# The decay mask of a Mamba-2 scan moved from ScalarE's bias and a masked score to eight VectorE instructions, with the ScalarE, VectorE and TensorE order around it rewritten

## The chip, the cores and the metric

The kernel runs on one core of a Trainium2 chip. A core has five engines that work at the same time: TensorE (PE; its weight loads are shown apart as PEld), VectorE (DVE), ScalarE (ACT), GpSimd (POOL) and SyncE (SP), which here only issues DMAs. Each engine takes its instructions in order and waits on semaphores for the others. The metric is the device time of one execution in microseconds (us). Lower is better.

## The reference, cut to what matters

The program is a chain of layers over 512 tokens of width 1024 in float32: a gated delta net, a chunked attention, two convolutional FFNs, an S5 mixer, an MLP, then the Mamba-2 mixer (`_ssd_mixer`) and another MLP. The change touches the Mamba-2 mixer alone. It has 4 chunks of 128 tokens and 32 heads in 4 groups of 8:

```python
a_cs = jnp.cumsum(a_dt, axis=-1)
l_mat = jnp.exp(_segsum(a_dt))          # exp(cs[l] - cs[s]) for s <= l, else 0
cb = jnp.einsum('bclgn,bcsgn->bcgls', c_in, b_in)
y_diag = jnp.einsum('bcgls,bgrcls,bcsgrp->bclgrp', cb, l_mat, xdt)
decay_states = jnp.exp(a_cs[..., -1:] - a_cs)
states = jnp.einsum('bclgn,bgrcl,bclgrp->bcgrpn', b_in, decay_states, xdt)
...
y_off = jnp.einsum('bclgn,bcgrpn,bgrcl->bclgrp', c_in, prev, jnp.exp(a_cs))
y = y_diag + y_off + xs * d.astype(f32).reshape(G, R, 1)
y = y.reshape(bsz, L, M2_D_INNER) * jax.nn.silu(z.astype(f32))
yg = y.reshape(bsz, L, G, M2_D_INNER // G)
yg = yg * lax.rsqrt(jnp.mean(yg * yg, axis=-1, keepdims=True) + NORM_EPS)
```

## The kernel before, in words

Every float32 product with a weight is three TensorE passes: the weight is split into a high part (ScalarE, L209, `w_hi`) and the rest (GpSimd, L238 or L2534, `w_lo`, two instructions of 128x1024 for one slot of weights). Weights stream through two buffers; SyncE issues their loads.

The scan is written out by hand as 16 steps, v = 0 to 15, where g = v // 4 is the group of heads and c = v % 4 the chunk. "c = 0" below means the steps 0, 4, 8, 12. Each engine has its own list of these steps.

TensorE (`ssd_pe`), in step v: `z_half(v)`, one 128-column tile of the gate projection z (24 matmuls of 512 columns, into bank v % 2); `pre(v + 1)`, which transposes the next step's x and B (L2460, L2465) and makes its scores C times B (L2466); `main(v)`, the 16 or 8 small products with `lw` (L2477) and `cdec` (L2479); and, but for c = 3, the new state (L2486). Around these stand parts of the norm of the group before: `gnorm_sums_pe` (L2652), the sums of squares of two tiles, after main(v) for c = 2 and 3, and `gnorm_spread_pe` (L2667), which spreads 1/rms over the partitions, ahead of main(v) for c = 1.

VectorE (`ssd_dve`): `xdt` (L2599, x times dt); then the difference `lw` (L2603), one instruction over 128x1024 that takes the minimum of the row of cumulated sums (`g_row`, the same row in every partition) and the partition's own sum; the outputs of step v - 1 (L2576); a wait for ScalarE; the triangular mask on the scores (L2613, 128x128 in PSUM); `lw` times scores (L2615); the state update of step v - 1 (L2588 or L2591). With c = 0 it multiplies the group before by silu(z) (`gnorm_gate_dve`, L2639); with c = 1 it makes 1/rms and scales the group before that (`gnorm_scale_dve`, L2675).

ScalarE (`ssd_act`): `b_tok` (L2505), `cdec` = exp of g_row (L2510), then eight exps of 128x128 on `lw`, each with the negated sum of its head as bias column (L2514). In the odd steps it then takes silu of two z tiles (L2520), splits the next slot of weights (L209), and for c = 1 and 2 squares two tiles of the group before (L2645). The root of the mean (L2658) comes after the exps of c = 0. Exp, silu and sqrt are in different tables of ScalarE; a change of table shows as ACT_TABLE_LOAD. Copy and Square need no change.

GpSimd (`ssd_pool`): decay of the state (L2545), `xdec` (L2556), `cdec` times C (L2562), and in the even steps from 2 on the two instructions of the low part of a slot (L2534).

SyncE loads `g_row` for step v once step v - 2 has used it; the weights of the output projection (`m_out`) come behind the last of these loads in its queue.

The minimum works as a mask because the cumulated sums fall with the token: where the row's token lies before the partition's, the minimum keeps the exponent at zero or below, and the triangle on the scores clears the entry.

Of the kernel before, what the change touches and what calls it, by code (L numbers as in the profile page):

```python
# [22 lines left out]
ALU = mybir.AluOpType  # L23
ACT = mybir.ActivationFunctionType
# [58 lines left out]
def ge(eng, sem, value):  # L83

    if isinstance(value, int) and value <= 0:
        return
    eng.wait_ge(sem, value)
# [19 lines left out]
def build(nc, t, out):  # L107

    ctx = ExitStack()
    with ctx:  # L110
# [2147 lines left out]
        g_in = [sem(f"g_in{i}") for i in range(2)]  # L2258
        M_NCS = 0
        (M_X, M_ABS, M_E, M_U, M_L, M_DT, M_ADT, M_CS, M_EDX, M_DEC) = range(10)  # L2260
# [93 lines left out]
        def steps_sums_dve(dve):  # L2354
            dve.wait_ge(d_pe, 1)
            dve.tensor_scalar(mcols[:, M_NCS, :], bank[7][:, 0:128], -1.0, None, ALU.mult)
            dve.tensor_copy(mcols[:, M_CS, :], bank[7][:, 0:128]).then_inc(d_dve, 1)
            dve.tensor_copy(mcols[:, M_DEC, :], bank[7][:, 128:256]).then_inc(d_dve, 1)
            dve.wait_ge(d_dve, 4)
            dve.tensor_tensor(mcols[:, M_EDX, :], mcols[:, M_DEC, :], mcols[:, M_CS, :], ALU.subtract).then_inc(d_dve, 1)  # L2360
# [46 lines left out]
        def z_slot(i):  # L2407
            return SLOTS["m_in"] + M_XBC + i
# [28 lines left out]
        def ssd_pe(pe):  # L2437
# [15 lines left out]
            def pre(v):  # L2453
# [7 lines left out]
                mm.then_inc(m_xt, 1)  # L2461
                ge(pe, m_w, 2 * (v - 1))
                ge(pe, m_bt, carried(v - 1) if v >= 2 else 0)
# [4 lines left out]
            def main(v):  # L2468
                g, c = v // 4, v % 4
                pe.wait_ge(m_w, 2 * v + 2)  # L2470
                if c:
# [16 lines left out]
            for v in range(16):  # L2488
                z_half(v)
                if v < 15:  # L2490
                    pre(v + 1)
                if v >= 8 and v % 4 == 1:
                    gnorm_spread_pe(pe, v // 4 - 2)
                main(v)
                if v >= 4 and v % 4 >= 2:
                    gnorm_sums_pe(pe, v // 4 - 1, v % 4 - 2)

        def ssd_act(act):
            for v in range(16):
# [11 lines left out]
                act.wait_ge(m_dl, v + 1)  # L2511
                for k in range(8):
                    col = c * M_H + 8 * g + k
                    op = act.activation(lw[v % 2][:, k, :], lw[v % 2][:, k, :], ACT.Exp, bias=mcols[:, M_NCS, col:col + 1])  # L2514
                op.then_inc(m_le, 1)
                if v % 2:
                    for z in (v - 1, v):
                        act.wait_ge(gemm_ready, 2 * z_slot(0) + z + 1)
                        ge(act, m_yz, z - 3)
                        act.activation(zT[:, z % 4, :], bank[z % 2][:, :], ACT.Silu).then_inc(bank_free, 1)  # L2520
                    n = z_slot(v // 2 + 2)
                    split_hi(act, n, n % 2, landed(n - n % 2))
                if g and c in (1, 2):
                    gnorm_squares_act(act, g - 1, c - 1)
                if g >= 2 and c == 0:
                    gnorm_root_act(act, g - 2)

# [39 lines left out]
        def ssd_dve(dve):  # L2567
# [25 lines left out]
            for v in range(16):  # L2593
                g, c = v // 4, v % 4
                dve.wait_ge(m_xt, v + 1)
                if v >= 2:
# [5 lines left out]
                dve.wait_ge(g_in[v % 2], 16 * (v // 2 + 1))  # L2602
                dve.tensor_tensor(lw[v % 2][:, :, :], g_row[v % 2][:, :, :],  # L2603
                                  mcols[:, M_CS, c * M_H + 8 * g:c * M_H + 8 * g + 8].unsqueeze(2).to_broadcast([P, 8, P]),
                                  ALU.min).then_inc(m_dl, 1)
                if v:
                    outputs(v - 1)
                if g >= 2 and c == 1:
                    gnorm_rcp_dve(dve, g - 2)
                dve.wait_ge(m_le, v + 1)  # L2610
                dve.wait_ge(m_cb, v + 1)
                scores = C_BANK[v % 2][:, P:2 * P]
                dve.tensor_tensor(scores, scores, triu[:, :], ALU.mult).then_inc(m_w, 1)  # L2613
                dve.wait_ge(m_w, 2 * v + 1)
                dve.tensor_tensor(lw[v % 2][:, :, :], lw[v % 2][:, :, :],  # L2615
                                  C_BANK[v % 2][:, P:2 * P].unsqueeze(1).to_broadcast([P, 8, P]), ALU.mult).then_inc(m_w, 1)
                if v:
                    states(v - 1)
                if g and c == 0:
                    gnorm_gate_dve(dve, g - 1)  # L2620
                if g >= 2 and c == 1:
                    gnorm_scale_dve(dve, g - 2)
            outputs(15)
            gnorm_rcp_dve(dve, 2)
            gnorm_gate_dve(dve, 3)
# [57 lines left out]
        def gnorm_act(act):  # L2683
            gnorm_root_act(act, 2)
            act.wait_ge(gemm_ready, 2 * SLOTS["m_out"])
            gnorm_hi_act(act, 0, 8)
            gnorm_squares_act(act, 3, 0)
            gnorm_squares_act(act, 3, 1)
            gnorm_root_act(act, 3)
            gnorm_hi_act(act, 8, 8)  # L2690
# [14 lines left out]
        def m_out_pe(pe):  # L2705
# [30 lines left out]
            pe.wait_ge(bank_free, 2 * base)  # L2736
            for k in range(2):
                first_pair(0, k)
            gnorm_spread_pe(pe, 2)
            for k in range(2, 6):  # L2740
                first_pair(0, k)
            gnorm_sums_pe(pe, 3, 0)
            for k in range(6, KD):
                first_pair(0, k)
# [308 lines left out]
```

## Time and profile before

| | |
|---|---|
| median of 3 runs | 3025.12 us (3024.24 to 3026.7) |
| the profiled execution's own time | 3026.7 us |
| its span, first to last instruction | 3024.9 us |
| busy: PE | 2856.2 us (94%) |
| busy: DVE, ACT, POOL | 1579.0, 1049.1, 1224.4 us |
| mean granted TensorE clock | 0.955 of full speed |
| the scan's 16 steps | about 2388 to 2548 us of the span |

Between the profiled execution's own time and its span lie 1.8 us at the two ends. Stretches are told in microseconds from the span's start. A busy share is an average over the whole program; what a change in the scan is worth is read from the stretch of the scan, and there from what TensorE waits for.

### The profile page before, as it was taken

The numbers are of one execution on the slowest core, as the hardware profiler recorded it, in microseconds if no ns is written. First come the engines' busy times: TensorE is split into PE (matmuls) and PEld (weight loads), VectorE is DVE, ScalarE is ACT, GpSimd is POOL, SyncE is SP. The second block draws the span as 40 slices with busy tenths as digits, with TensorE's granted clock in tenths as the row PEclk, the third lists the DMA queues.
The fourth block names the chain that finished last, engine by engine and source line by source line (L and its number), as shares of the span: only waits on it lengthen the run. The fifth ranks groups of instructions, "written<-read, shape, count | busy, mean of one in ns | idle before, by whom it ended". The sixth has DMA issues, their size and how long they took to land.

```text
span 3024.9 us, 38804 instructions
## 1 busy us (share of the span) xinstructions
PE 2856.2 (94%) x14541; PEld 2345.6 (78%) x14541; DVE 1579.0 (52%) x2180; ACT 1049.1 (35%) x1425; POOL 1224.4 (40%) x556
## 2 busy tenths in 40 slices
PE   7999999999998998999998789999999998999998
PEld 6867886788877865788886677888878787778887
DVE  4435655676768447564556626555354465242224
ACT  4331222333333246333333212222224666232222
POOL 3433432344444420344443214444433566544443
PEclk9998998999999989999998779999999999999999
DMA  4320000335532320455533732655322332223322
GB/s 133 94 76 22 1 1 14 112 95 148 154 116 85 111 99 29 137 171 170 189 117 116 236 101 83 236 195 181 98 83 87 111 107 77 84 84 98 98 98 70
DMA packets 343960, 326.43 MB, mean 108 GB/s; under 512 B 28816, under 2 KB 320144, under 8 KB 343696
## 3 DMA queue, kind: packets, MB, share of 16 engines
q1 hardware_dynamic: 309760, 257.34, 27.4%
q10 hardware_dynamic: 34064, 67.18, 6.3%
q8 instruction: 97, 1.59, 0.2%
q14 instruction: 39, 0.32, 0.0%
HBM read 303.44 MB, written 21.04 MB: 107 GB/s over the span
## 4 chain that ended last, share of the span: by engine, by line
PE 72%; DVE 6%; issue 3%; ACT 3%; POOL 1%; DMA 0%; ACTq 0%; DVEq 0%; SPq 0%; POOLq 0%
PE bank L248 18%; PE bank L250 18%; PE bank L249 18%; PE bank L262 3%; PE bank L267 3%; PE bank L263 3%; PE bank L1923 1%; PE bank L1918 1%; PE bank L1347 1%; PE bank L363 1%; DVE xt L406 0%; DVE sq_x L333 0%; PE bank L679 0%; PE bank L2652 0%; PE bank L2477 0%
## 5 line engine op out<-in xcount | busy, mean ns | idle before, releaser
L238 POOL TENSOR_TENSOR w_lo<-w_raw,w_hi 128x1024 fp32r<-128x1024 f32 x400 | 1009.3, 2545 | 1459.6 <-ACT w_hi L209 1444.1
L248 PE MATMUL bank<-x_hi,w_hi 128*128 128x512 f32 x2032 | 799.8, 394 | 12.7 <-POOL w_lo L238 7.8
L249 PE MATMUL bank<-x_lo,w_hi 128*128 128x512 f32 x2032 | 793.3, 390 | 0.0
L250 PE MATMUL bank<-x_hi,w_lo 128*128 128x512 f32 x2032 | 793.2, 390 | 0.0
L209 ACT ACTIVATE w_hi<-w_raw 128x2048 fp32r<-128x2048 f32 x208 | 398.1, 1914 | 892.5 <-PE bank L250 792.0
L248 PEld LDWEIGHTS bank<-x_hi,w_hi 128*128 128x128 f32 x2032 | 383.3, 189 | 96.9 <-issue 15.2
L249 PEld LDWEIGHTS bank<-x_lo,w_hi 128*128 128x128 f32 x2032 | 383.4, 189 | 81.0 <-issue 2.2
L250 PEld LDWEIGHTS bank<-x_hi,w_lo 128*128 128x128 f32 x2032 | 383.1, 189 | 80.3
L248 PE MATMUL bank<-m_hi,w_hi 128*128 128x512 f32 x384 | 149.6, 390 | 0.0
L250 PE MATMUL bank<-m_hi,w_lo 128*128 128x512 f32 x384 | 149.4, 389 | 0.0
L249 PE MATMUL bank<-m_lo,w_hi 128*128 128x512 f32 x384 | 149.4, 389 | 0.0
L1212 DVE SCALAR_TENSOR_TENSOR y_gate<-bank,par,y_gate 128x511 f32<-128x511 f32 x88 | 66.0, 750 | 155.6 <-ACT y_gate L1146 153.9
L2231 DVE SCALAR_TENSOR_TENSOR h<-bank,mod,h 128x512 f32<-128x512 f32 (+1 forms) x64 | 47.4, 749 | 183.0 <-PE bank L250 166.1
L2210 DVE SCALAR_TENSOR_TENSOR m_r<-bank,m_r 128x512 f32<-128x512 f32 x64 | 43.8, 684 | 178.4 <-ACT m_r L2163 178.4
L1062 DVE SCALAR_TENSOR_TENSOR ada_acc<-ada_w,cond,ada_acc 128x1024 f32<-128x1024 f32 (+1 forms) x84 | 119.7, 1425 | 1.6
L2214 DVE TENSOR_TENSOR m_lo<-m_r,m_hi 128x512 fp32r<-128x512 f32 (+1 forms) x64 | 78.9, 1233 | 52.2 <-ACT m_hi L2165 52.2
L248 PE MATMUL bank<-act_hi,w_hi 128*128 128x512 f32 x264 | 103.2, 391 | 0.0
L250 PE MATMUL bank<-act_hi,w_lo 128*128 128x512 f32 x264 | 102.7, 389 | 0.0
L249 PE MATMUL bank<-act_lo,w_hi 128*128 128x512 f32 x264 | 102.7, 389 | 0.0
L262 PE MATMUL bank<-x_hi,w_hi 128*128 128x512 f32 x176 | 79.6, 452 | 18.3 <-ACT x_hi L373 8.1
L574 DVE SCALAR_TENSOR_TENSOR qkvz<-bank,par,qkvz 128x511 f32 (+2 forms) x72 | 53.8, 749 | 77.4 <-ACT qkvz L544 67.8
L838 POOL TENSOR_TENSOR X<-Rm,lev 128x512 f32<-128x512 f32 x56 | 70.3, 1270 | 54.4 <-PE bank L784 47.8
(436 smaller groups left out, 4642.3 us busy)
## 6 DMA issues: line engine op xcount, KB each, us to landing
w_raw<-in_mlp_w SPq DMA_DIRECT2D x128, 512.0 KB, 4.5
ada_w<-in_ada_w ACTq DMA_DIRECT2D x96, 512.0 KB, 4.9
w_raw<-in_f_w_up SPq DMA_DIRECT2D x88, 512.0 KB, 5.1
w_raw<-in_m_w_in SPq DMA_DIRECT2D x40, 512.0 KB, 4.7
w_raw<-in_a_w_in SPq DMA_DIRECT2D x32, 512.0 KB, 4.7
w_raw<-in_f_w_down SPq DMA_DIRECT2D x32, 512.0 KB, 4.0
w_raw<-in_w_kv SPq DMA_DIRECT2D x16, 512.0 KB, 4.3
w_raw<-in_s_w_glu SPq DMA_DIRECT2D x16, 512.0 KB, 5.4
```

The lines of the kernel that those rows point to most:

```text
L209: act.activation(w_hi[s][:, :], w_raw[s][:, :], ACT.Copy).then_inc(hi_done, 1)
L238: op = pool.tensor_tensor(w_lo[s][:, part], w_raw[s][:, part], w_hi[s][:, part].bitcast(F32), ALU.subtract)
L248: pe.matmul(dst, hi_l, hi_r, start=start, stop=False)
L249: pe.matmul(dst, hi_l, lo_r, start=False, stop=False)
L250: return pe.matmul(dst, lo_l, hi_r, start=False, stop=stop)
L262: pe.matmul(bank[o][:, :], w_hi[0][:, cols[o]], rhs_hi[:, k, :], start=(k == 0), stop=False)
L263: pe.matmul(bank[o][:, :], w_lo[0][:, cols[o]], rhs_hi[:, k, :], start=False, stop=False)
L267: mm = pe.matmul(bank[o][:, :], w_hi[0][:, cols[o]], rhs_lo[:, k, :], start=False, stop=(k == kt - 1))
L838: pool.tensor_tensor(X2[s][:, :, :], Rm[s][:, :, :], bc4(lev[:, l, :]), ALU.mult).then_inc(da_mask, 1)
L1062: dve.scalar_tensor_tensor(acc, ada_w[k][:, :, :], cond[:, k:k + 1], acc, ALU.mult, ALU.add).then_inc(ada_used, 1)
L1212: dve.scalar_tensor_tensor(y[:, s, d:T], bank[2 * s + o][:, 0:T - d], pcol("f_conv", i + (3 * 44 * f + 44 * (2 - d) + col + F_START[c] + s ...
L2214: dve.tensor_tensor(lo, m_r[:, o, :], m_hi[:, ds(2 * i + (2 * s + o), 1), :].bitcast(F32), ALU.subtract).then_inc(p_lo, 1)
```

## The change

The mask goes into the exponent. VectorE takes, head by head, row minus the head's own sum plus `upmask` (0 on and above the diagonal, -1e30 below), eight instructions of 128x128, and ScalarE then needs one exp of 128x1024 with no bias. The minimum, the triangle on the scores and the column of negated sums (`M_NCS`) go. The order of the rest changes too: silu of z is taken in every step, not for two tiles in every other; the squares' sums on TensorE stand after main(v) of c = 1 and 2; root, reciprocal and spread of the group before stand at the end of c = 3; scale and gate stand together in c = 0; and the first products of the output projection no longer hold a spread.

```diff
 def steps_sums_dve(dve):
-    dve.tensor_scalar(mcols[:, M_NCS, :], bank[7][:, 0:128], -1.0, None, ALU.mult)
...
 ssd_pe, in step v
-                if v >= 8 and v % 4 == 1:
-                    gnorm_spread_pe(pe, v // 4 - 2)
                 main(v)
-                if v >= 4 and v % 4 >= 2:
-                    gnorm_sums_pe(pe, v // 4 - 1, v % 4 - 2)
+                if v >= 4 and v % 4 in (1, 2):
+                    gnorm_sums_pe(pe, v // 4 - 1, v % 4 - 1)
+                if v >= 4 and v % 4 == 3:
+                    gnorm_spread_pe(pe, v // 4 - 1)
...
 ssd_act, in step v
                 act.wait_ge(m_dl, v + 1)
-                for k in range(8):
-                    col = c * M_H + 8 * g + k
-                    op = act.activation(lw[v % 2][:, k, :], lw[v % 2][:, k, :], ACT.Exp, bias=mcols[:, M_NCS, col:col + 1])
-                op.then_inc(m_le, 1)
+                act.activation(lw[v % 2][:, :, :], lw[v % 2][:, :, :], ACT.Exp).then_inc(m_le, 1)
+                act.wait_ge(gemm_ready, 2 * z_slot(0) + v + 1)
+                ge(act, m_yz, v - 3)
+                act.activation(zT[:, v % 4, :], bank[v % 2][:, :], ACT.Silu).then_inc(bank_free, 1)
                 if v % 2:
-                    for z in (v - 1, v):
-                        act.wait_ge(gemm_ready, 2 * z_slot(0) + z + 1)
-                        ge(act, m_yz, z - 3)
-                        act.activation(zT[:, z % 4, :], bank[z % 2][:, :], ACT.Silu).then_inc(bank_free, 1)
                     n = z_slot(v // 2 + 2)
                     split_hi(act, n, n % 2, landed(n - n % 2))
                 if g and c in (1, 2):
                     gnorm_squares_act(act, g - 1, c - 1)
-                if g >= 2 and c == 0:
-                    gnorm_root_act(act, g - 2)
+                if g and c == 3:
+                    gnorm_root_act(act, g - 1)
...
 ssd_dve, in step v
-                dve.tensor_tensor(lw[v % 2][:, :, :], g_row[v % 2][:, :, :],
-                                  mcols[:, M_CS, c * M_H + 8 * g:c * M_H + 8 * g + 8].unsqueeze(2).to_broadcast([P, 8, P]),
-                                  ALU.min).then_inc(m_dl, 1)
+                for k in range(8):
+                    op = dve.scalar_tensor_tensor(lw[v % 2][:, k, :], g_row[v % 2][:, k, :],
+                                                  mcols[:, M_CS, c * M_H + 8 * g + k:c * M_H + 8 * g + k + 1], upmask[:, :],
+                                                  ALU.subtract, ALU.add)
+                op.then_inc(m_dl, 1)
                 if v:
                     outputs(v - 1)
-                if g >= 2 and c == 1:
-                    gnorm_rcp_dve(dve, g - 2)
                 dve.wait_ge(m_le, v + 1)
                 dve.wait_ge(m_cb, v + 1)
-                scores = C_BANK[v % 2][:, P:2 * P]
-                dve.tensor_tensor(scores, scores, triu[:, :], ALU.mult).then_inc(m_w, 1)
-                dve.wait_ge(m_w, 2 * v + 1)
                 dve.tensor_tensor(lw[v % 2][:, :, :], lw[v % 2][:, :, :],
                                   C_BANK[v % 2][:, P:2 * P].unsqueeze(1).to_broadcast([P, 8, P]), ALU.mult).then_inc(m_w, 1)
                 if v:
                     states(v - 1)
-                if g and c == 0:
+                if v >= 4 and c == 0:
+                    if g >= 2:
+                        gnorm_scale_dve(dve, g - 2)
                     gnorm_gate_dve(dve, g - 1)
-                if g >= 2 and c == 1:
-                    gnorm_scale_dve(dve, g - 2)
+                if g and c == 3:
+                    gnorm_rcp_dve(dve, g - 1)
             outputs(15)
-            gnorm_rcp_dve(dve, 2)
...
 gnorm_act
-            gnorm_root_act(act, 2)
...
 m_out_pe
-            for k in range(2):
-                first_pair(0, k)
-            gnorm_spread_pe(pe, 2)
-            for k in range(2, 6):
+            for k in range(4):
                 first_pair(0, k)
             gnorm_sums_pe(pe, 3, 0)
-            for k in range(6, KD):
+            for k in range(4, KD):
                 first_pair(0, k)
```

The waits on `m_w` count one increment for each step in place of two.

## Rows read from the trace of the kernel before

**Rows 1.** The waits, 2385 to 2590 us: who waited for whom, us, times, longest.

```profile
DVE bank L2613 <- ACT lw L2514: 47.7, 16, 5.6
...
PEld bank L2477 <- DVE lw L2615: 5.9, 3, 3.6
...
PE bank L2477 <- DVE prev L2591: 5.5, 4, 3.4
```

**Rows 2.** Timeline of TensorE: start, us, engine, line, output and inputs, count.

```profile
2413.91 0.45 PE L2477 MATMUL bank<-lw,xdt 128*64 128x128 f32 x4
...
2423.15 0.45 PE L2477 MATMUL bank<-lw,xdt 128*64 128x128 f32 x4
...
2431.53 1.09 PE L2477 MATMUL bank<-lw,xdt 128*64 128x128 f32 x16
...
2439.85 0.45 PE L2477 MATMUL bank<-lw,xdt 128*64 128x128 f32 x4
...
2452.82 1.84 PE L2652 MATMUL bank<-ones,sq 128*128 128x1 f32 x16
...
2479.69 1.06 PE L2667 MATMUL bank<-ident,ncol 128*128 128x128 f32 x8
...
2533.35 0.45 PE L2477 MATMUL bank<-lw,xdt 128*64 128x128 f32 x4 [3.40 <-DVE prev L2591]
```

**Rows 3.** Timeline of ScalarE, steps 5 and 6.

```profile
2437.05 1.28 ACT L2520 ACT_TABLE_LOAD   x1
2438.35 0.60 ACT L2520 ACTIVATE zT<-bank 128x512 f32<-128x512 f32 x1
...
2439.68 1.91 ACT L209 ACTIVATE w_hi<-w_raw 128x2048 fp32r<-128x2048 f32 x1
2441.48 1.14 ACT L2645 ACTIVATE sq<-xbc 128x512 f32<-128x512 f32 x2
...
2444.10 1.06 ACT L2510 ACTIVATE cdec<-g_row 128x1024 f32<-128x1024 f32 x1
2445.07 2.43 ACT L2514 ACTIVATE lw<-lw,mcols 128x128 f32<-128x128 f32 x8
```

**Rows 4.** Timeline of VectorE, in steps 4, 6 and 9.

```profile
2430.33 2.49 DVE L2639 SCALAR_TENSOR_TENSOR xbc<-xbc,zT 128x512 f32<-128x512 f32 x4
...
2439.62 0.69 DVE L2599 TENSOR_TENSOR xdt<-bank,mcols 128x512 f32<-128x512 f32 x1 [0.39 <-PE bank L2460]
2440.23 1.22 DVE L2603 TENSOR_TENSOR lw<-g_row,mcols 128x1024 f32<-128x1024 f32 x1
...
2447.53 0.30 DVE L2613 TENSOR_TENSOR bank<-bank,triu 128x128 f32<-128x128 f32 x1 [4.51 <-ACT lw L2514]
2447.87 1.22 DVE L2615 TENSOR_TENSOR lw<-lw,bank 128x1024 f32<-128x1024 f32 x1
...
2480.79 2.72 DVE L2675 SCALAR_TENSOR_TENSOR xbc<-xbc,par,bank 128x512 f32<-128x512 f32 x4 [2.02 <-PE bank L2667]
```

**Rows 5.** Timeline of GpSimd, in step 6.

```profile
2442.95 1.04 POOL L2556 TENSOR_TENSOR xdec<-xdt,mcols 128x512 f32<-128x512 f32 x1
2445.24 2.40 POOL L2562 TENSOR_TENSOR cdec<-cdec,xbc 128x1024 f32<-128x1024 f32 x1 [1.25 <-ACT cdec L2510]
```

**Rows 6.** Timelines of VectorE, then GpSimd, in the S5 tables, 966 to 1003 us.

```profile
970.53 2.39 DVE L1771 SCALAR_TENSOR_TENSOR tab<-tab,scol 128x64 f32<-128x64 f32 x1
972.85 2.43 DVE L1772 SCALAR_TENSOR_TENSOR tab_tmp<-tab,scol 128x64 f32<-128x64 f32 x1
...
977.14 0.29 DVE L1771 SCALAR_TENSOR_TENSOR tab<-tab,scol 128x128 f32<-128x128 f32 x1
977.35 0.28 DVE L1772 SCALAR_TENSOR_TENSOR tab_tmp<-tab,scol 128x128 f32<-128x128 f32 x1
...
970.45 4.74 POOL L238 TENSOR_TENSOR w_lo<-w_raw,w_hi 128x1024 fp32r<-128x1024 f32 x2 [20.31 <-ACT w_hi L209]
```

**Rows 7.** The chain that ended last, 2370 to 2620 us: start, us, what.

```profile
2515.60 7.45 DMA w_raw<-in_m_w_out
```

More of the change, by code:

```diff
@@ L2258, in build @@
         g_in = [sem(f"g_in{i}") for i in range(2)]
-        M_NCS = 0
         (M_X, M_ABS, M_E, M_U, M_L, M_DT, M_ADT, M_CS, M_EDX, M_DEC) = range(10)
@@ L2461, in pre @@
                 mm.then_inc(m_xt, 1)
-                ge(pe, m_w, 2 * (v - 1))
+                ge(pe, m_w, v - 1)
                 ge(pe, m_bt, carried(v - 1) if v >= 2 else 0)
@@ L2469, in main @@
                 g, c = v // 4, v % 4
-                pe.wait_ge(m_w, 2 * v + 2)
+                pe.wait_ge(m_w, v + 1)
                 if c:
```

## The prediction, made before the changed kernel was run

> **What bounds the kernel now.** I read the page first: TensorE is busy 94% of the span, so in the scan I asked only what TensorE waits for. The waits of that stretch [rows 1] show the large number on VectorE, 47.7 us of waiting for ScalarE's exps, and small ones on TensorE: 5.5 us in four places for the updated state and, at three of the same places, 5.9 us for `lw`. So the long wait of VectorE is nearly all hidden behind `z_half`. The timeline of TensorE gives the undisturbed period of a step, main to main [rows 2]: 9.24 us for c = 2 to 3 (2413.91 to 2423.15), 8.38 for c = 3 to 0, 8.32 for c = 0 to 1. I take 9.24 for c = 1 to 2 also. From group 1 on come two sums of 1.7 to 1.8 us and one spread of some 0.9. The waits lie in steps 6, 7, 10, 11, 14 and 15, where the starts of main are 6 to 6.5 us late in all, against these periods; 3.4 of it stand ahead of main(14) [rows 2], behind a weight load that the chain shows as 7.45 us [rows 7]. At most about 6 us can be won inside the scan.
>
> **The change part by part.** The eight exps took 2.43 us; one exp over 128x1024 has its nearest row in `cdec`, 1.06 [rows 3]: 1.4 us less on ScalarE. The mask goes: 0.34 us from its start to that of the product [rows 4]. The negated column is one small VectorE instruction, once, some 0.3 us by the mask's row, and nothing waits closely for it.
>
> The difference costs more. A pair of `scalar_tensor_tensor` of 128x128 with both tensors in SBUF stands at 977.14 and 977.35 [rows 6]: 0.21 us apart, the last 0.29, so eight take 7 x 0.21 + 0.29 = 1.76 us, against 1.22 [rows 4]. If nothing else acts, `lw` times scores is ready 1.4 + 0.34 - 0.54 = 1.2 us earlier in each step.
>
> Something else acts. At 970.45 GpSimd starts two w_lo instructions, 4.74 us together. VectorE's two instructions of 128x64, with no wait between them in the code, then take 2.39 and 2.43 us in place of some 0.2: the first stands until GpSimd's first is over, and the second until GpSimd's second is over [rows 6]. They take turns, one instruction each. One long instruction loses one such turn; eight short ones can lose a turn to every instruction that GpSimd has ready. The Trainium skill ("SBUF — State Buffer", "SBUF: two separate sides") says that a VectorE instruction with two SBUF inputs and a GpSimd instruction that reads SBUF exclude each other for the whole instruction, whichever starts first; it doesn't say who gets the port at a boundary between short ones. The trace agrees on the exclusion.
>
> What GpSimd has ready comes from its order. `xdec`, 1.04 us, is released by the xdt just ahead of the difference; `cdec` takes 2.40 [rows 5], a w_lo pair 4.74. I place the turns, from measured durations.
>
> Steps with c = 1: xdec, then cdec: difference 1.76 + 1.04 + 2.40 = 5.2 us. In step 5 the way from the product of step 4 is the four gates (2.4), xdt (0.6), difference (5.2), exp (1.1), product (1.25) and state (0.65), 11.1 us in all [rows 3, 4], against a period of 8.32: TensorE waits 2.8. In steps 9 and 13 the scale now stands there too, 2.6: 13.7 against 8.32, 5.4 us each. Sum 13.6.
>
> Steps 4, 8, 12: xdec and both w_lo: 1.76 + 1.04 + 4.74 = 7.5 us, and with exp and product main is ready 10.1 us after the difference starts. In steps 8 and 12 the difference also starts late, since VectorE now waits for the root: ScalarE does silu (0.5), the split (1.9), a table load (1.3) and the root (0.3) first [rows 3]. I get waits of 3.1, 3.1, and 2.1 in step 4. Sum 8.3.
>
> Steps 0 and 3: one w_lo in step 0; the decay of the state and cdec in step 3 between the short ones: 1.35 and 1.5. Sum 2.9.
>
> The spread: it needs root and reciprocal, about 4.4 us after the silu of z, which starts 0.66 ahead of main; so 3.75 after main's start, and main takes 2.0: 1.75 us of waiting in steps 7 and 11. In step 15 it lies ahead of the first y_lo, which starts some 8 us after main(15) in either kernel, and is hidden. Sum 3.5.
>
> Step 13: the squares stand behind the split of the late weight load [rows 3, 7], and their sums now come before z_half(14): 0.8. In return the old wait at main(14) goes.
>
> Moved sums and spreads: one pair of sums (1.8) is now ahead of main(15) that stood in cover behind it, and one spread (0.9) leaves the output projection: +0.9.
>
> The sum: 13.6 + 8.3 + 2.9 + 3.5 + 0.8 + 0.9 - 6.3 (the old waits) = +23.7 us. The profiled execution took 3026.7, so 3050.4; it is 1.6 above the median of the runs, so 3049 us for the median, about 0.8% slower. GpSimd's own work is unchanged; ScalarE saves 1.4 x 16 = 22 us and pays up to 16 more table loads of 1.3 us, 21 us, in places where it otherwise waits.
>
> Table loads: the trace has 1.28 us for the load and 1.30 from its start to that of the silu behind it [rows 3]. The Trainium skill ("ScalarE: Activation LUTs", "What ACT_TABLE_LOAD costs") counts about 2.66 us for a switch, with a drain of 1.38. By that figure root and spread would come 1.4 us later in steps 7 and 11, an estimate of 3 us more. The trace has no such drain, and the sum goes by its row.
>
> Bounds of the unknown terms. Where each turn falls: if no turn is lost the waits of steps 0, 3, 4 and 5 vanish and those of 8, 9, 12 and 13 too (the way in step 9 is 13.7 - 3.4 = 10.3 from product to main, and the earlier product leaves it in cover), which takes off 24.8. If a second cdec or w_lo turn falls into two more steps it adds 2.4 each. TensorE's clock: after idle time it can fall to the lower of its two levels; 3.4 us ahead of main(14) left it at full speed, and 5.4 is longer than that. What lies ahead of a drop I bound by none and by 2 us for each of steps 9 and 13.
>
> **The rivals.** (1) No change that can be told. The eight short instructions hold the port like one. For it: they are issued back to back with no wait, and the difference is only 0.54 us longer then. Against it: the pair at 970.53 had no wait between them either and lost a turn each. Then the sum is 23.7 - 24.8 = -1: 3024 us.
>
> (2) Faster. ScalarE's order decides: with exps 1.4 us shorter and squares a step earlier, the waits of steps 6, 7, 10, 11, 14 and 15 go, 6.3 us, the spread leaves the projection, 0.9, and root and reciprocal come in time. Place: steps 7 and 11, where the root would have to be done by main's end. Price: -7.2, 3018 us. It decides if turns are kept and the way from silu to spread is under 2.7 us; against it stand 4.4 from the rows.
>
> (3) Slower by half of it: GpSimd wins a turn only when its next instruction is already queued, as at 970.45 (a pair), and not with a fresh xdec or cdec. Then the c = 0 steps keep their waits in part and c = 1 lose them: about 8.3 + 3.5 + 0.8 + 0.9 - 6.3 plus 2 for step 9 and 13, +9: 3034 us.
>
> **How the numbers follow.** The turns as I placed them: 0.60, 3049 us, own range 3040 to 3060. (3): 0.20, 3029 to 3040. (1): 0.13. (2): 0.07. A change under about 0.2%, 6 us, can't be told from none by this measurement. Faster 0.07; same 0.13; a tenth of (3) would fall into it too, so 0.15; slower 0.78. The range leaves out (2) and half of (1) below, 0.07 and 0.06, and 0.05 above: 3024 to 3060.
>
> **What the profile of the changed kernel would show.** The instructions of `lw<-g_row,mcols,upmask`, 128 of them, with 0.29 us as their least and some of 1.3 and 2.6 us, between which xdec, cdec or w_lo of GpSimd run; the difference as a whole near 5 us for c = 1 and 7.5 for c = 0. One exp of 1.06. TensorE waiting for `lw` or the state of steps 3, 4, 5, 8, 9, 12 and 13, longest at 9 and 13, and 1.7 us ahead of the spread in steps 7 and 11; no wait ahead of main(14). About 16 more table loads. The start of the output projection some 22 us later than 2549. If the 128 instructions all take 0.29, the turns are wrong and the time is near that of before; if waits ahead of the spread are missing too, (2) holds. The prediction is also wrong where GpSimd's work falls at other times than I placed it, since two steps of lateness move which instruction is ready.

## The result, and the profile after

| | before | after |
|---|---|---|
| median of the runs compared | 3024.68 us (3022.64 to 3026.7, 4 runs) | 3058.62 us (3050.95 to 3060.2, 4 runs) |
| the profiled execution's own time | 3026.7 us | 3054.83 us |
| its span | 3024.9 us | 3053.0 us |
| from the first `xdt` of the scan to the first `h` of the output projection | 194.69 us | 225.90 us |

The ratio is 1.0108, with a 95% interval of 1.0096 to 1.0119: the change makes the kernel 1.1% slower, by 29 to 36 us. All 31 runs on record of the kernel after have a median of 3057.39 us (3050.95 to 3061.96), so the 33.9 us between the two medians of the table, which the text below uses, may be some 1 us too large. 3049 us had been predicted, in a range of 3024 to 3060. The last row of the table is the part of the program that the change touches, measured in the two traces; it grew by 31.2 us. The span grew by 28.1 only, because the part ahead of the scan, whose code is the same, was 4.05 us shorter in this execution (the first `xdt` starts at 2384.44 and not at 2388.49). For the scan I therefore compare this stretch and not the span; it is called the scan time below.

The page of the kernel after, its span and the busy times:

```profile
span 3053.0 us, 38801 instructions
PE 2869.6 (94%) x14541; PEld 2357.7 (77%) x14541; DVE 1620.6 (53%) x2275; ACT 1044.9 (34%) x1327; POOL 1212.2 (40%) x556
```

TensorE is as busy as before, 94%, and gained only 13 us of busy time. VectorE gained 42 us. So I asked again what TensorE waits for. The waits of the kernel after, 2381 to 2611 us (who waited for whom: us, times, longest):

```profile
ACT lw L2510 <- DVE lw L2598: 40.7, 10, 6.6
...
PEld bank L2475 <- DVE lw L2606: 19.6, 7, 4.0
...
DVE lw L2606 <- ACT lw L2510: 13.5, 5, 5.5
...
PE bank L2475 <- DVE prev L2582: 10.7, 4, 3.8
...
PE bank L2475 <- DVE lw L2606: 6.9, 3, 2.7
...
PEld bank L2659 <- DVE ncol L2654: 6.2, 3, 2.6
```

In [rows 1] VectorE waited 47.7 us for ScalarE; now ScalarE waits 40.7 us for VectorE's difference. TensorE's matmuls waited 5.5 us for the state, in four places; now 10.7 for the state and 6.9 for `lw`, and its weight loads, which stand just ahead of them, 19.6 for `lw` in place of 5.9. The spread, which did not wait [rows 2], waits three times, in the steps 7, 11 and 15.

The difference itself, by the instructions that touch `lw` (x count: shortest, median, longest in ns):

```profile
L2598 DVE SCALAR_TENSOR_TENSOR lw<-g_row,mcols,upmask x128: 336/343/2485, 2385.0 to 2563.0; 128x128 f32<-128x128 f32 x128
L2510 ACT ACTIVATE lw<-lw x16: 1038/1057/1064, 2390.5 to 2564.1; 128x1024 f32<-128x1024 f32 x16
```

The median of the 128 short instructions is 0.343 us and the longest 2.485, about GpSimd's product for `cdec` [rows 5]. Each of the 16 exps takes the 1.06 us that was expected. The timelines of VectorE and GpSimd show the turns. Step 8, then step 9:

```profile
2470.16 7.24 DVE L2598 SCALAR_TENSOR_TENSOR lw<-g_row,mcols,upmask 128x128 f32<-128x128 f32 x8
...
2485.30 5.09 DVE L2598 SCALAR_TENSOR_TENSOR lw<-g_row,mcols,upmask 128x128 f32<-128x128 f32 x8
...
2493.85 2.18 DVE L2598 SCALAR_TENSOR_TENSOR lw<-g_row,mcols,upmask 128x128 f32<-128x128 f32 x8
```

```profile
2470.32 1.08 POOL L2550 TENSOR_TENSOR xdec<-xdt,mcols 128x512 f32<-128x512 f32 x1 [9.35 <-DVE xdt L2593]
2471.36 4.84 POOL L2528 TENSOR_TENSOR w_lo<-w_raw,w_hi 128x1024 fp32r<-128x1024 f32 x2
...
2485.46 1.08 POOL L2550 TENSOR_TENSOR xdec<-xdt,mcols 128x512 f32<-128x512 f32 x1 [9.26 <-DVE xdt L2593]
2487.57 2.41 POOL L2556 TENSOR_TENSOR cdec<-cdec,xbc 128x1024 f32<-128x1024 f32 x1 [1.02 <-ACT cdec L2508]
```

In step 10 (2493.85) GpSimd starts nothing until the last of the eight is under way (its next instruction starts at 2495.66): 2.18 us. In step 9 xdec and cdec fall between them: 5.09, and in step 8 xdec and the two w_lo: 7.24. The prediction had 5.2 and 7.5 for these two kinds.

What it does to TensorE (its timeline):

```profile
2442.48 0.45 PE L2475 MATMUL bank<-lw,xdt 128*64 128x128 f32 x4 [2.79 <-DVE prev L2582]
...
2469.67 1.16 PE L2659 MATMUL bank<-ident,ncol 128*128 128x128 f32 x8 [1.56 <-DVE ncol L2654]
...
2479.80 1.09 PE L2475 MATMUL bank<-lw,xdt 128*64 128x128 f32 x16 [2.70 <-DVE lw L2606]
...
2493.59 0.45 PE L2475 MATMUL bank<-lw,xdt 128*64 128x128 f32 x4 [3.80 <-DVE prev L2582]
...
2549.35 3.28 PE L2644 MATMUL bank<-ones,sq 128*128 128x1 f32 x16 [1.74 <-ACT sq L2637]
...
2560.66 0.45 PE L2475 MATMUL bank<-lw,xdt 128*64 128x128 f32 x4
```

From one main to the next, by their starts, the periods in us are:

| step to next | 0 | 1 | 2 | 3 | 4 | 5 | 6 | 7 | 8 | 9 | 10 | 11 | 12 | 13 | 14 |
|---|---|---|---|---|---|---|---|---|---|---|---|---|---|---|---|
| before | 8.31 | 9.14 | 9.24 | 8.38 | 8.32 | 10.09 | 11.36 | 10.17 | 9.21 | 9.49 | 11.19 | 10.17 | 9.21 | 12.61 | 11.18 |
| after | 8.72 | 9.13 | 10.35 | 9.91 | 11.17 | 12.56 | 11.05 | 13.71 | 13.79 | 10.89 | 11.05 | 13.71 | 13.80 | 17.62 | 10.27 |

The columns 5, 9 and 13 of the kernel after also hold a pair of sums (1.8 us) that stood two steps later before. The losses stand where the prediction put them (at main(3) to main(5), main(8), main(9), main(12) and main(13)) and in one place where it had almost none: between main(13) and main(14), 17.62 us.

### The profile page after: what moved, and what is told of

Same layout as the page of the kernel before. It is cut to its first block, busy times and chain, and to the rows that moved or that the text cites. A ratio compares the mean times of both kernels' runs of the same rounds, so it can differ in the third digit from the quotient of the medians.

```text
span 3053.0 us, 38801 instructions
## 1 busy us (share of the span) xinstructions
PE 2869.6 (94%) x14541; PEld 2357.7 (77%) x14541; DVE 1620.6 (53%) x2275; ACT 1044.9 (34%) x1327; POOL 1212.2 (40%) x556
## 4 chain that ended last, share of the span: by engine, by line
PE 70%; DVE 8%; issue 3%; ACT 2%; DMA 0%; POOL 0%; ACTq 0%; DVEq 0%; SPq 0%; POOLq 0%
PE bank L248 18%; PE bank L250 18%; PE bank L249 18%; PE bank L262 3%; PE bank L267 3%; PE bank L263 3%; DVE lw L2598 1%; PE bank L1923 1%; PE bank L1918 1%; PE bank L1347 1%; PE bank L363 1%; PE bank L2644 1%; DVE xt L406 0%; PE bank L679 0%; DVE sq_x L333 0%
## 5 line engine op out<-in xcount | busy, mean ns | idle before, releaser
L238 POOL TENSOR_TENSOR w_lo<-w_raw,w_hi 128x1024 fp32r<-128x1024 f32 x400 | 1007.3, 2540 | 1455.4 <-ACT w_hi L209 1439.9
```

Source lines behind the costliest of these rows:

```text
L238: op = pool.tensor_tensor(w_lo[s][:, part], w_raw[s][:, part], w_hi[s][:, part].bitcast(F32), ALU.subtract)
```

## The experiments

All medians are set against runs of the kernel before on the same chip. The scan time is that of each profiled execution.

| kernel | median, us | less before | ratio (95%) | scan time less that of before |
|---|---|---|---|---|
| after | 3058.62 | +33.9 | 1.0108 (1.0096 to 1.0119) | +31.2 |
| old order, new arithmetic | 3036.26 | +9.9 | 1.0040 (1.0027 to 1.0052) | +10.5 |
| new order, old arithmetic | 3036.43 | +10.1 | 1.0038 (1.0024 to 1.0052) | +13.4 |
| after, GpSimd held back | 3034.27 | +7.9 | 1.0028 (1.0018 to 1.0038) | +11.2 |
| after, two long instructions | 3041.13 | +14.8 | 1.0052 (1.0035 to 1.0068) | +16.6 |
| after, mask in PSUM | 3032.05 | +6.6 | 1.0018 (1.0009 to 1.0027) | +10.2 |
| after, early load | 3053.80 | +28.4 | 1.0087 (1.0071 to 1.0102) | +27.8 |
| after, held back, early load | 3027.70 | +2.3 | 1.0006 (0.9996 to 1.0015) | +2.8 |
| the same, and an early root | 3019.69 | -5.6 | 0.9978 (0.9969 to 0.9988) | -3.3 |
| old order, new arithmetic, held back | 3020.68 | -4.8 | 0.9984 (0.9975 to 0.9994) | -2.6 |
| the same, and early load | 3019.00 | -6.3 | 0.9980 (0.9970 to 0.9990) | -2.8 |
| before, early load alone | 3020.45 | -4.8 | 0.9985 (0.9976 to 0.9994) | -3.3 |

### The turns: GpSimd held back by one wait

```diff
 ssd_pool, in step v, behind the decay of the state, ahead of xdec
+                pool.wait_ge(m_dl, v + 1)
```

> The changed kernel with one more wait: in each step GpSimd starts xdec, cdec and the weights' low part only once the eight short VectorE instructions of the difference are done. Nothing is computed otherwise. Theory T (turns: each short instruction loses the port to a GpSimd instruction that is ready): all but the first of the eight go back to about 0.2 us apart, the difference takes 1.8 us in most steps, TensorE's waits of 2.7 to 3.8 us in steps 5, 8, 9, 12 and 13 go, and the time falls by some 25 to 32 us, to 3023 to 3031. Rival O (the new order with its root, spread, scale, gate and table loads costs the time): GpSimd's work is only later, the time stays at 3050 or above. Rival L (the eight instructions' own length, 1.8 in place of 1.2 us): it stays too, since there are still eight.

It took 3034.27 us. Against before that is +7.9 us in place of +33.9: 26 us given back by the medians, and 20.0 by the scan times of the two traces. The instructions of VectorE and GpSimd are the same; only the time at which GpSimd starts is another. VectorE's timeline of this kernel in step 9, then GpSimd's:

```profile
2474.63 2.17 DVE L2599 SCALAR_TENSOR_TENSOR lw<-g_row,mcols,upmask 128x128 f32<-128x128 f32 x8
```

```profile
2476.89 1.05 POOL L2551 TENSOR_TENSOR xdec<-xdt,mcols 128x512 f32<-128x512 f32 x1 [5.13 <-DVE lw L2599]
2477.89 2.37 POOL L2557 TENSOR_TENSOR cdec<-cdec,xbc 128x1024 f32<-128x1024 f32 x1
```

The difference now takes 2.17 in step 9 and 2.18 in step 8, and the periods 7 to 8 and 8 to 9 fall from 13.71 and 13.79 to 10.93 and 9.74. That is the turns. The result lies 3 us above the top of what I had expected, and the trace says where: the period 13 to 14 is not shorter but longer, 18.79. The wait has a price of its own: `cdec` is now late at two mains, 2.7 us in all.

### Is it the port? The mask from PSUM

```diff
+            for b in range(2):
+                dve.tensor_copy(C_BANK[b][:, 2 * P:3 * P], upmask[:, :]).then_inc(m_mk, 1)
...
 ssd_dve, in step v
+                dve.wait_ge(m_cb, v + 1)
+                if c < 3:
+                    dve.wait_ge(m_bt, carried(v) + 1)
                 for k in range(8):
                     op = dve.scalar_tensor_tensor(lw[v % 2][:, k, :], g_row[v % 2][:, k, :],
-                                                  mcols[...], upmask[:, :],
+                                                  mcols[...], C_BANK[v % 2][:, 2 * P:3 * P],
                                                   ALU.subtract, ALU.add)
```

A copy of the mask stands in unused columns of the two score banks. The two waits keep VectorE from reading a bank that TensorE is writing. GpSimd's order is that of the kernel after.

> The changed kernel with its mask read from PSUM: a copy of upmask stands in the free columns of the two score banks, so that each of the eight short instructions has one tensor in SBUF and one in PSUM. GpSimd's order isn't touched; the difference now waits for the scores and b_tok of its step. T (two SBUF inputs are what makes VectorE and GpSimd exclude each other): no turn is lost, the eight take 2.1 to 2.5 us in every step while GpSimd's xdec and cdec run beside them at 1.04 and 2.4 us, and the time is near that of the hold, 3028 to 3038. Rival P (it is the number of short instructions, or their semaphores, that costs): no gain, 3055.

It took 3032.05 us: +6.6 in place of +33.9, 27 us given back by the medians and 21.0 by the scan times. The instructions on `lw` in this kernel, then VectorE's difference of step 9, then GpSimd in the same stretch:

```profile
L2607 DVE SCALAR_TENSOR_TENSOR lw<-g_row,mcols,bank x128: 336/343/349, 2383.7 to 2539.9; 128x128 f32<-128x128 f32 x128
```

```profile
2470.94 2.15 DVE L2607 SCALAR_TENSOR_TENSOR lw<-g_row,mcols,bank 128x128 f32<-128x128 f32 x8
```

```profile
2471.10 1.04 POOL L2552 TENSOR_TENSOR xdec<-xdt,mcols 128x512 f32<-128x512 f32 x1 [4.28 <-DVE xdt L2599]
2473.20 2.40 POOL L2558 TENSOR_TENSOR cdec<-cdec,xbc 128x1024 f32<-128x1024 f32 x1 [1.06 <-ACT cdec L2510]
```

xdec runs in the middle of the eight, as in the kernel after, and neither loses anything: the longest of 128 instructions falls from 2485 to 349 ns. The same instruction with one of its two tensors in PSUM does not take turns with GpSimd. The Trainium skill ("SBUF — State Buffer", "SBUF: two separate sides") names two SBUF inputs as a condition for the exclusion; this run agrees. The two added waits cost this kernel something too: in six steps VectorE's difference waits for `b_tok`, 16.4 us in all; in step 9, shown here, it does not.

### Few long instructions in place of many short ones

```diff
-                for k in range(8):
-                    op = dve.scalar_tensor_tensor(..., ALU.subtract, ALU.add)
-                op.then_inc(m_dl, 1)
+                dve.tensor_tensor(lw[v % 2][:, :, :], g_row[v % 2][:, :, :], mcols[...].to_broadcast([P, 8, P]),
+                                  ALU.subtract).then_inc(m_d1, 1)
+                dve.wait_ge(m_d1, v + 1)
+                dve.tensor_tensor(lw[v % 2][:, :, :], lw[v % 2][:, :, :],
+                                  upmask[:, :].unsqueeze(1).to_broadcast([P, 8, P]), ALU.add).then_inc(m_dl, 1)
```

> The changed kernel with its difference in two long instructions in place of eight short ones: subtract the own sums over 128x1024, then add the mask over 128x1024. The same values, 2.4 us of VectorE alone in place of 1.8, but only two turns to lose. T: in a c = 1 step the difference takes 2.4 + 1.0 (xdec) = 3.5 us in place of 5.1, in c = 0 about 3.5 to 5.8 in place of 7.2; the time is 8 to 20 us below the changed kernel, 3036 to 3048. L: longer arithmetic makes it slower than the changed kernel, by up to 0.6 us a step: 3060 or more. O: no change or slightly slower.

It took 3041.13 us, +14.8 in place of +33.9: 19 us given back by the medians and 14.6 by the scan times, though without contention two instructions of 1.22 us are longer than the eight together. VectorE's timeline, step 9:

```profile
2476.46 1.21 DVE L2598 TENSOR_TENSOR lw<-g_row,mcols 128x1024 f32<-128x1024 f32 x1
2477.70 1.95 DVE L2602 TENSOR_TENSOR lw<-lw,upmask 128x1024 f32<-128x1024 f32 x1
```

From start to end this is 3.19 us, against 5.09. GpSimd gets one turn between the two, and its work waits in return (that xdec stands at 1.96 us in place of 1.04). So in this kernel the loss goes with the number of boundaries between VectorE's instructions, not with the work.

### Order and arithmetic apart

The kernel before with the new difference and the one exp, and without the mask on the scores; the order of all engines is the old one:

```diff
-                dve.tensor_tensor(lw[v % 2][:, :, :], g_row[v % 2][:, :, :], mcols[...].to_broadcast([P, 8, P]), ALU.min).then_inc(m_dl, 1)
+                for k in range(8):
+                    op = dve.scalar_tensor_tensor(lw[v % 2][:, k, :], g_row[v % 2][:, k, :], mcols[...], upmask[:, :], ALU.subtract, ALU.add)
+                op.then_inc(m_dl, 1)
```

> The kernel before with the arithmetic of the change alone: eight short instructions with the mask, one exp, no triangle on the scores; the order of all engines as before. T: turns are lost here as well (the difference takes about 5 us for c = 1 and 7 for c = 0), but scale and gate stand in different steps and VectorE doesn't wait for the root, so most of it lies in cover: waits of 1 to 2 us in steps 3, 4, 5, 10 and 14, less about 3 us that shorter exps save: +2 to +8 us against the kernel before, 3027 to 3033. O: the arithmetic saves 1.2 us a step on the way to main, so the time is 3 to 6 us below before. L: about +1.

The other half, the new order with the minimum, eight exps and the mask on the scores:

```diff
 ssd_act, in step v
+                act.wait_ge(gemm_ready, 2 * z_slot(0) + v + 1)
+                ge(act, m_yz, v - 3)
+                act.activation(zT[:, v % 4, :], bank[v % 2][:, :], ACT.Silu).then_inc(bank_free, 1)
...
-                if g >= 2 and c == 0:
-                    gnorm_root_act(act, g - 2)
+                if g and c == 3:
+                    gnorm_root_act(act, g - 1)
```

> The changed kernel with the arithmetic of before: one minimum, eight exps with bias, triangle on the scores; the order of the change. T: only the spread's waits (1.6 us in steps 7 and 11) and some 1.6 us in steps 9 and 13 are added, and moved sums: +4 to +10 us against before, 3029 to 3035. O: nearly all of the loss is here, +25 or more, 3050. L: as T.

They took 3036.26 and 3036.43 us: each half costs about 10. Both came out above what was expected, the arithmetic by 2 to 3 us and the order at the very edge of its range; the difference of the arithmetic alone took 7.06 us in step 3 and 7.24 in step 4. Together the halves make 20 and the whole change 33.9; by the scan times they make 23.9 and the whole 31.2. The periods show where the 7.3 us between these two come from:

| step to next | 7 | 8 | 11 | 12 | 13 |
|---|---|---|---|---|---|
| before | 10.17 | 9.21 | 10.17 | 9.21 | 12.61 |
| new arithmetic, old order | 10.17 | 11.00 | 10.17 | 11.00 | 12.30 |
| old arithmetic, new order | 10.91 | 10.97 | 10.90 | 10.99 | 16.24 |
| after | 13.71 | 13.79 | 13.71 | 13.80 | 17.62 |

In the old order the 7.2 us of step 8 lie in cover (10.17, as before). The new order lets VectorE wait for 1/rms and gives it scale and gate in the same step, so the cover is used up, and each further microsecond of VectorE is one of TensorE. In the periods 7, 8, 11 and 12 the whole change costs 7.7 us more than the two halves added up. The medians differ by more, 14; no row shows the other 6 us.

### The arithmetic with the old order, held back

```diff
 the kernel before with the new arithmetic, ssd_pool, ahead of xdec
+                pool.wait_ge(m_dl, v + 1)
```

> The kernel before, with the arithmetic of the change and GpSimd held until the difference is done; the order of the other engines as before. T: the difference takes 2.2 us in place of 1.2, exp 1.4 less, the mask 0.3 less, no turns; main(6), (7), (10), (11) and (15) start without their waits of 0.3 to 1.1 us, main(14) 1.7 us earlier, step 0 0.8 later: 2 to 5 us below the kernel before. L: no gain, within 1 us of it.

3020.68 us, 4.8 below before, as expected; its scan time is 2.6 less. The new arithmetic is a gain, if a small one, once the turns are gone.

### The long period 13 to 14: the late weight load

The chain that ended last, in the kernel after (start, us, what); then ScalarE's timeline:

```profile
2539.86 0.32 SPq L2422
...
2540.51 0.40 SPq L171
...
2541.10 5.66 DMA w_raw<-in_m_w_out
...
2548.59 0.62 ACT sq L2637
```

```profile
2546.78 1.91 ACT L209 ACTIVATE w_hi<-w_raw 128x2048 fp32r<-128x2048 f32 x1 [3.94 <-DMA w_raw<-in_m_w_out]
2548.59 1.13 ACT L2637 ACTIVATE sq<-xbc 128x512 f32<-128x512 f32 x2
```

SyncE takes the load of `g_row` for step 15 (L2422) only when the difference of step 13 has ended, and the weights of the output projection stand behind it. The difference of step 13 ends 5.09 us after it starts, late, so the load, the split and the squares come late, and TensorE waits 1.74 us for the squares. The chain after it has z matmuls of 0.43 us in place of 0.23, and the windows show the granted clock (of each stretch: us, busy times, then the clock, the DMA share and GB/s):

```profile
2540.00:2550.00 10.00, 5.22 (x39) 4.28 (x39) 6.51 (x19) 6.01 (x8) 2.04 (x2) 0.81 0.80 262
2550.00:2560.00 10.00, 10.00 (x38) 8.48 (x38) 1.82 (x2) 4.47 (x4) 7.06 (x3) 0.68 0.01 2
```

The edit that tests it puts the first load of the output projection ahead of the `g_row` loads of steps 14 and 15 in SyncE's queue:

```diff
+            sp_slot(sp, z_slot(8), halves(rows_k(t["m2_w_out"][0]), 0, 0, KD, 0))
...
-            sp_slots(sp, SLOTS["m_out"], 8, lambda i, s: halves(w, s, (i - s) * P, KD, KD * s))
+            (the same loads, without the first)
```

> The changed kernel with one load moved in SyncE's queue: the first slot of the output projection's weights ahead of the g_row loads of steps 14 and 15, in place of behind them. Theory T2 (the late load is what makes step 13 to 14 take 17.6 us in place of 11: it stands behind the g_row load of step 15, and that waits for the difference of step 13): the split of step 13 no longer waits, step 13 to 14 falls to about 11 to 12 us, the clock doesn't fall there, and the time is 5 to 7 us below the changed kernel, 3050 to 3053. Rival: the 3.8 us wait ahead of main(13) alone brings the clock down, and the slow matmuls, not the load, make up the time: 1 to 3 us.

3053.8 us, 0.8 above the expected range; the period 13 to 14 falls from 17.62 to 12.41, and no other moves by more than 0.04. One part of the expectation failed: the clock still falls at main(13). Windows within this period show it, of the kernel after, of this one, and of the held-back kernel with the same early load, which comes next:

```profile
2544.00:2546.00 2.00, 2.00 (x22) 2.00 (x21) 1.47 (x6) 0.00 (x0) 0.00 (x0) 0.50 1.08 375
...
2550.00:2556.00 6.00, 6.00 (x21) 5.29 (x21) 1.82 (x2) 4.47 (x4) 3.67 (x2) 0.50 0.01 3
```

```profile
2546.00:2548.00 2.00, 2.00 (x22) 2.00 (x21) 2.00 (x9) 2.00 (x3) 0.00 (x0) 0.50 1.04 365
2549.00:2558.00 9.00, 9.00 (x52) 7.36 (x48) 2.95 (x7) 4.54 (x5) 8.71 (x5) 1.00 0.01 4
```

```profile
2522.00:2533.00 11.00, 10.62 (x79) 8.98 (x80) 5.35 (x15) 7.69 (x9) 8.04 (x6) 1.00 0.29 101
```

In the kernel after the granted clock is at the lower of its two levels twice: in main(13), behind the wait of 3.82 us, and again behind the 1.74 us for the squares. The early load takes away that second wait and the slow matmuls behind it, 5.2 us together. It leaves the first drop, in which the rival of the expectation was right: 12.41 us against 10.90 in the kernel whose clock stays up, 1.5 us.

Against before the kernel is +28.4 in place of +33.9, and the scan time falls by 3.5: of the 5.2 us won here, 1.7 are gone again by the first `h`. The granted clock was 0.83 in 2572 to 2592, where the kernel after has 0.91; that would make 1.6 us, but no run tests it. The same edit in the kernel with GpSimd held back:

> Both: GpSimd held until the difference is done (as in the run with the hold alone, 3034.3) and the load moved ahead. T2: step 13 to 14 falls from 18.8 to about 11 us, so 3025 to 3029. Rival: 3031 or more.

3027.7 us, +2.3 in place of the +7.9 of the kernel that is only held back; the scan time falls by 8.4. There the period had been 18.79, and TensorE waited 4.64 us for the squares, where in the kernel after it is 1.74. That this is because the steps stand closer together, so that TensorE has less to do while the load is under way, was not tested. ScalarE's and TensorE's timelines of the held-back kernel:

```profile
2528.09 1.91 ACT L209 ACTIVATE w_hi<-w_raw 128x2048 fp32r<-128x2048 f32 x1 [5.65 <-DMA w_raw<-in_m_w_out]
```

```profile
2530.66 3.55 PE L2645 MATMUL bank<-ones,sq 128*128 128x1 f32 x16 [4.64 <-ACT sq L2638]
```

With the early load the period is 10.90. In every kernel of the new order whose load was left where it is the period is long: 16.24 with the old arithmetic, 20.44 with the two long instructions, 19.85 with the mask in PSUM. Against the 12.61 of before that is 6.2 of the 11.2 us of scan time that the held-back kernel still loses, 7.2 of 10.2 with the mask in PSUM and 7.8 of 16.6 with the two long instructions. And in the kernel before, alone:

> The kernel before with the early load alone. T: the 3.4 us ahead of main(14) fall to about 1 us, as ahead of main(10): 2 to 3 us less than before. Rival: no change.

3020.45 us, 4.8 less, its interval 0.06% to 0.24%. Expected were 2 to 3. The period 13 to 14 falls from 12.61 to 9.50, which is 3.1 of the 3.3 us by which the scan time falls.

### The spread: an early root

```diff
 the kernel held back with early load, ssd_act, c = 3
                 act.activation(lw[v % 2][:, :, :], lw[v % 2][:, :, :], ACT.Exp).then_inc(m_le, 1)
+                if g and c == 3:
+                    gnorm_root_act(act, g - 1)
                 act.wait_ge(gemm_ready, 2 * z_slot(0) + v + 1)
                 act.activation(zT[:, v % 4, :], bank[v % 2][:, :], ACT.Silu).then_inc(bank_free, 1)
...
-                if g and c == 3:
-                    gnorm_root_act(act, g - 1)
```

> The kernel with the hold and the early load (3027.7), and the root of the norm taken before silu of z and the split of the weights in the steps 7, 11 and 15. T: TensorE's waits of 1.6 to 1.8 us ahead of the spread in steps 7 and 11 go, and the difference of steps 8 and 12 starts earlier: 3 to 5 us less, 3023 to 3025. Rival: the spread's waits were cover for work that then waits elsewhere: under 1 us.

3019.69 us, -5.6 against before in place of +2.3: 7.9 us, where some 3 to 5 had been expected; the scan time falls by 6.05. ScalarE's timeline of this kernel in step 7, then TensorE's:

```profile
2456.13 1.28 ACT L2652 ACT_TABLE_LOAD   x1
2457.43 0.27 ACT L2652 ACTIVATE ncol<-bank,eps_col 128x4 f32<-128x4 f32 x1
```

```profile
2463.83 1.16 PE L2661 MATMUL bank<-ident,ncol 128*128 128x128 f32 x8
```

The root is done 3.5 us before silu starts, in time in which ScalarE waited for z, and the spread no longer waits. It is more than the spread's own wait: 7 to 8 falls from 10.93 to 9.27, 1.66, and 8 to 9 from 9.71 to 8.31, another 1.4, because VectorE, whose reciprocal and `xdt` stood behind the root, is earlier too. Twice 3.06 is 6.1, the whole of it.

The arithmetic in the old order, held back, with the early load, stands beside it:

> The arithmetic of the change in the order of before, with the hold (3020.7) and the early load. T: the wait ahead of main(14), which the hold alone leaves at 1.7 us or more, goes as well: 3017 to 3020. Rival: the squares behind the split hold step 14 all the same: no change.

3019.0 us, inside the expected range, but this is no proof of the step that was named: without the early load the period 13 to 14 was 9.53 already, with it 9.14, and the scan times, 2.6 and 2.8 us below before, can't be told apart.

## Why the prediction was right, and where it was off

**What bounds the kernel** held: VectorE became the one that TensorE waits for, at the steps named.

**The difference.** I had 1.76 us for the eight undisturbed, from a spacing of 0.21 and a last one of 0.29. Measured: 2.18, seven times 0.26 and 0.34. The pair of [rows 6] is another form of the instruction and understated it by 0.4 us. With the turns 5.2 and 7.5 were predicted, 5.09 to 5.11 and 7.24 to 7.25 measured, in steps 1, 5, 9 and 13 and in steps 4, 8 and 12. Step 3, where other work of GpSimd fell in, took 6.65. Turns also fell where the prediction had placed fewer or none: step 0 took 5.47 us and step 11 took 5.85. The one in step 11 cost TensorE nothing (its period is 11.05 with and without the turns); the loss at main(0), 0.79, is the same 0.8 in the kernel with GpSimd held back, so it isn't shown to be the turns'.

**The turns** were the main step, and are shown: a wait on GpSimd that changes no work took 26 us out of the kernel; one operand in another memory took out 27, with GpSimd's order left alone; fewer boundaries took out 19. By the scan times it is 20.0, 21.0 and 14.6. The prediction had 24.8 for all turns. The held-back kernel pays 2.7 for the late `cdec` and 1.2 more in the period 13 to 14, and 20.0 with these two makes 23.9, an estimate. Rival (3), in which a fresh xdec wins no turn, fell in the first trace: at 2485.46 a fresh xdec stands between the short ones.

**Steps 5, 9 and 13**: periods predicted 11.1, 13.7 and 13.7; measured 11.17, 13.79 and 13.80. (The six parts of the first add up to 11.2.) TensorE's wait in steps 9 and 13 was 3.80 and 3.82, not 5.4, since the clock had fallen behind main(8) and main(12) and its z matmuls took the rest; VectorE sets the period, so the time is the same. **Steps 4, 8 and 12**: periods predicted by the stated waits 10.5, and some 14.1 with spread and its wait; measured 9.91, 13.71 and 13.71. **Steps 0 and 3**: predicted 1.35 and 1.5; measured 1.2 (0.79 at the first main and 0.41 in the next period) and 1.11. **The spread** waited 1.56 at 2469.67, predicted 1.75. In step 15 it waited 2.32, and that was hidden as said: with the early root the wait is gone, and main(15) to the first `h` takes 39.35 us in place of 39.32. **Main(14)** has no wait ahead of it, as said.

**Step 13** is the term of the sum that was mis-sized. The squares' wait stood there with 0.8, and TensorE's clock with nothing. The period came out at 17.62, against 11.7 by my terms (9.14 undisturbed, as measured between main(1) and main(2), where I had taken 9.24; 1.8 for the sums, 0.8): 5.9 us short. I had kept the load's length [rows 7] and had not asked what its issue waits for. It waits, through the `g_row` load ahead of it in SyncE's queue, for the difference of step 13, the very instruction that I had lengthened from 1.2 to 5.2 and delayed. The early load took 5.2 us out of this period in the kernel after, a wait of 1.74 for the squares and the slow matmuls behind it, and 7.9 in the held-back one. The other 1.5 us are the drop of the clock at main(13), which the early load leaves. 5.2 and 1.5, less the 0.8 that I had counted, are the 5.9.

**The clock** I had bounded at 0 to 2 us for steps 9 and 13 and not put into the sum. At main(9), behind 3.80 us of wait, it stayed at its upper level. At main(13) it fell and cost 1.5, inside the bound. It also fell where I had not looked: in main(5), behind 2.79 us (0.83 in 2440 to 2450), where the period 5 to 6 is 12.56 against 10.94 (1.6 us), and behind the squares' wait of step 14 (0.68 in 2550 to 2560). The 5.9 of step 13 and the 1.6 of main(5) are the 7.5 by which the scan time (+31.2) passed the sum (+23.7); the rest cancels.

The measured time lies 9.6 us above the forecast of 3049 and 1.4 below the top of the range. That it lies inside is owed to the width of the range and not to a term for either of these two.

**The rival "no turn lost"** was costed at 3024. The held-back kernel is that case and took 3034.27: the mechanism of the rival would have been right and its time 10 us wrong, for the same missing term (the period 13 to 14 is 18.79) and for the 2.7 us of the late `cdec`. With the early load it is 3027.7. The faster rival (2) asked for turns kept and a root in time; with both brought about by hand, and the early load, 3019.69 was measured and 3018 had been its price. That is not a verdict for the change: the kernel before with the early load alone, 3020.45, can't be told from it, and neither can the new arithmetic in the old order, 3019.0.

**Table loads** cost what the row showed, and 14 came on top where up to 16 had been said: ScalarE has 98 instructions fewer, with 112 exps gone. Load and next start are 1.29 to 1.30 us apart (2456.13 to 2457.43), and no drain of 1.38 shows behind any that I read; the Trainium skill's 2.66 for a switch ("ScalarE: Activation LUTs", "What ACT_TABLE_LOAD costs") is not what this trace has.

Open is the rest between the medians (+33.9) and the scan (+31.2); it lies inside the interval of the ratio, and nothing was run on it. Open too is why the medians give the experiments up to 6 us more than the scan times do (26 against 20.0 for the held-back kernel): each scan time is that of one execution, the medians are of several, and those of the experiments come from three chips. Why the arithmetic in the old order cost more than expected was not taken apart further.

## What to carry to other kernels

Before one VectorE instruction on two SBUF tensors is cut into several short ones, look at what GpSimd has ready in that stretch: each boundary can give it a turn of the whole length of its next instruction. Hold it back by a wait, keep the instruction whole, or put one operand into PSUM; of the 31.2 us of scan time a wait took back 20.0 here, PSUM 21.0, and two long instructions in place of eight short ones 14.6. And when an instruction gets longer, follow its semaphore into the DMA queues as well: a load that stands behind one that waits for it is late by the same amount, and may be exposed a step later, where nothing was changed.

## What the runs showed of the hardware that was not expected

Eight `scalar_tensor_tensor` of 128x128 with a column as their scalar follow each other at 0.26 us; the pair of [rows 6], whose scalar is the constant 1.0, stands 0.21 apart.

The length of a wait alone does not tell whether TensorE's granted clock falls. TensorE's timeline at main(13) of the kernel after:

```profile
2543.04 0.70 PE L2475 MATMUL bank<-lw,xdt 128*64 128x128 f32 x4 [3.82 <-DVE prev L2582]
```

The four took 0.70 us, behind 3.82 us of wait; at main(9) the same four took 0.45, behind 3.80. The granted clock was 1.00 in 2490 to 2500, around the one, and 0.81 in 2540 to 2550, around the other. It also fell behind main(8), with 2.70 us of wait (0.83 in 2480 to 2490), and behind main(12), with 2.72 (0.87 in 2530 to 2540); there the drop cost nothing, since VectorE set the length of these steps.
